# Three edits of issue order in an encoder trunk: key copies, a modulation sum, low parts of activations

## The chip, the cores and the metric

The kernel runs on one core of one Trainium2 chip. The metric is the device time of one execution in microseconds (us). The engines are TensorE (PE), VectorE (DVE), ScalarE (ACT), GpSimd (POOL) and SyncE (SP). Each works through its own instruction stream strictly in order and waits on semaphores for the others.

## The reference

Two encoder layers over 256 tokens of width 1024, float32. Every sub-layer works on a normed and modulated stream, and its output returns through a gate. Only the first layer's attention and the start of its channel mixer matter here:

```python
mod = silu(c) @ ada_w[l] + ada_b[l]
sh_a, sc_a, g_a, sh_f, sc_f, g_f = jnp.split(mod, 6, axis=-1)
h = modulate(rms_norm(x, norm_attn[l]), sh_a, sc_a)
# differential attention, 8 heads, two softmax maps each
q, k, v = split(h @ w_qkv);  q = rms_norm(q) / 8;  k = rms_norm(k)
p = softmax(q k^T + bias)                    # two maps: p[0], p[1]
o = (p[0] - lam * p[1]) @ v
y = (rms_norm(o) * (1 - lam_init)).reshape(...) @ w_o
x = x + g_a * y
h = modulate(rms_norm(x, norm_ffn[l]), sh_f, sc_f)
x = x + g_f * (silu(h @ w_in_gate) * (h @ w_in_up)) @ w_out
```

After this come a shared key and value projection, a layer of sliding-window attention and a mixture of 8 experts (top 2), which takes some two thirds of the time.

## The kernel before

**Units and split products.** All weights stream through a ring of 12 raw slots of 128x1024 float32 (`WRAW`), loaded by SP. One slot's content is a unit. ACT copies a unit, rounded, to `WHI` (`hi`, line 697) and DVE subtracts to get the low part `WLO` (`lo`, line 1080). Each product is three matmuls (`split_mm`): high by high, high by low, low by high. There are 6 split slots, so `hi(k)` waits until TensorE has used unit k-6, and a raw slot is loaded again when `lo` of its unit is done. The activations, transposed by TensorE into PSUM, are split the same way: `ht_his` on ACT (line 756), `ht_los` on DVE (line 1153 or 1155).

**Unit numbers.** 0 to 7 are the query weights, 8 to 15 key, 16 to 23 value, 24 to 31 the output weights, 32 to 35 the first input weights of the dense channel mixer, 36 to 39 the next, 40 and 41 its first output weights.

**Around the key copies.** TensorE runs value units 16 to 18, transposes the normed queries, runs 19 and 20, transposes the normed keys, runs 21, waits for all eight copies (`qkt_ready`, 8), computes the logits of heads 0 and 1, then unit 22, logits 2, unit 23, logits 3, and enters the attention (line 1931). The copies are `transposed(...)` on ACT (line 764). ACT copies the values to SBUF (line 802) once unit 23 is used; the first probabilities times values need them. On DVE, `biased(n)` (lines 1186 and 1190) adds the bias to head n's logits and takes the negated maximum; `totals(n)` (lines 1200 to 1206) forms the difference of maps. A block of queries is 128 rows; heads 0 to 7 of block 0 come first, then those of block 1. DVE also sums the modulation rows, one `early_product` per 128x1024 piece of `ada_w` (line 1094); eight of them, (3, 0) to (3, 7), give the shift of the channel mixer, of which the last two come after `lo(31)`.

**Around the shift sum.** `project_by_block` multiplies the attention output by units 24 to 31. Its order is (block, unit): (0,0) to (0,4), (1,0), (1,1), (0,5), (0,6), (0,7), (1,2) to (1,7). `between` names what TensorE does behind such a step. `shift_sum` waits for the last early product (`DVE_EARLY`) and sums the shift over partitions by a matmul with ones; ACT copies the result (`mod_rows`, line 741) ahead of `hi(32)`, the norm root of block 0 and `hi(33, 34)`. `block_out` after (0,7) releases `residual(0)` on DVE (lines 1235 and 1236), then `scaled`, `rms`, `norm` (line 1142). Behind (1,6) TensorE transposes that normed block.

**Into the channel mixer.** TensorE runs units 32 to 35 for block 0, transposes block 1's normed rows (line 1744, behind `norm(1)`), runs 32 to 35 for block 1, then 36 and 37 (`f_in_first`), transposes the activation, and goes on with 38 and 39, 40 and 41, 42 and on. POOL waits for the second half of `norm(1)` (`h_ready`, 12), clears a part of `MOD` (line 622), loads biases and a gain, and then the pieces of the later modulation matrices into the four slots of `SHR` (line 573). DVE multiplies them between its `lo` operations (`late_products`, line 1105): the first two stand ahead of `lo(38)`.

Of the kernel before, what the change touches and what calls it, by code (L numbers as in the profile page):

```python
# [20 lines left out]
ACT = mybir.ActivationFunctionType  # L21
# [30 lines left out]
U_QKV = 0  # L52
# [118 lines left out]
def trunk(nc, t):  # L171
    ctx = ExitStack()
    with ctx:
# [3 lines left out]
        def sem(name):  # L177
            return ctx.enter_context(nc.semaphore(name))
# [51 lines left out]
        K = MOD[:, 7:9, :]  # L230
# [8 lines left out]
        def s_buf(a, n):  # L239

            n = n % S_BUFS
            if a == "B":
                buf = B_BUFS[:, n * B_BUF:n * B_BUF + 2 * BIAS_COLS] if n < 3 else GB[:, 0:2 * BIAS_COLS]
                return buf.rearrange("p (m k) -> p m k", m=2)
            if n < 2:
                return S[:, n, :, :]
            return MOD[:, 5, :].rearrange("p (n m k) -> p n m k", n=2, m=2)[:, n - 2, :, :]
# [79 lines left out]
        qkt_psum = sem("qkt_psum")  # L327
# [357 lines left out]
        def _(act):  # L685
# [5 lines left out]
            def hi(u, *units):  # L691
                for k in units:
                    act.wait_ge(w_landed[u.raw(k)], u.landed(k))
                    if u.first + k >= SPLIT_SLOTS:

                        act.wait_ge(w_used, u.count(k - SPLIT_SLOTS) + 1)
                    nc.scalar.activation(WHI[:, u.split(k), :], WRAW[:, u.raw(k), :], ACT.Copy  # L697
                                         ).then_inc(w_hi, 1)
# [15 lines left out]
            def load_table(func):  # L714

                n = tables[0]
                tables[0] += 1
                nc.scalar.activation(rt[:, 7, n:n + 1], ones[:, 0:1], func)
# [42 lines left out]
            def transposed(first, dst_of, col, banks, total):  # L761
                for n, bank in enumerate(banks):
                    act.wait_ge(total, first + n + 1)
                    nc.scalar.activation(dst_of(n), PS[:, bank, :], ACT.Copy, scale=gcol[:, col:col + 1]
                                         ).then_inc(qkt_ready if total is qkt_psum else kbt_ready, 1)

            def attention(a, early=None, between=None):
                sems = attn[a]

                def exps(n):  # L770
                    i, span = n // HEADS, (n // HEADS + 1) * P
                    act.wait_ge(sems["negmax"], n + 1)
                    buf, c = s_buf(a, n), sm[:, n % S_BUFS, :]
                    cols = span if a == "A" else span + 1
                    for m in range(2):
                        nc.scalar.activation(buf[:, m, 0:cols], buf[:, m, 0:cols], ACT.Exp,
                                             bias=c[:, 2 + m:3 + m],
                                             accum_out=c[:, 4 + m:5 + m]).then_inc(sems["expd"], 1)

                def copy_pt(n):  # L780
                    maps = 1 if a == "A" else 2
                    span = (n // HEADS + 1) * P
                    act.wait_ge(sems["pt_psum"], n + 1)
                    if n >= 2:
                        act.wait_ge(sems["pv"], n - 1)
                    nc.scalar.activation(PT[:, n % 2, 0:maps, 0:span],
                                         PS[:, 4 + n % 2, :].rearrange("p (m k) -> p m k", m=2)[:, 0:maps, 0:span],
                                         ACT.Copy).then_inc(sems["pt_ready"], 1)

                def copy_o(n):  # L790
                    i, h = n // HEADS, n % HEADS
                    act.wait_ge(sems["pv"], n + 1)
                    nc.scalar.activation(Q[:, i, h * P:(h + 1) * P], PS[:, 6, 0:P], ACT.Copy,
                                         scale=sm[:, n % S_BUFS, 8:9]).then_inc(sems["o_ready"], 1)

                n_all = TB * HEADS
                exps(0)
                exps(1)
                if a == "A":
                    act.wait_ge(w_used, U_WO)  # L800
                    for i in range(TB):
                        nc.scalar.activation(V[:, i, :], pair(4 + 2 * i), ACT.Copy).then_inc(v_copied, 1)
                for n in range(n_all):
                    if n + 2 < n_all:
                        exps(n + 2)
                    copy_pt(n)
                    if n and a == "A":
                        copy_o(n - 1)
                    if n in (1, 2) and a == "B":
                        transposed(9 + n, lambda _: Q[:, 1, (n - 1) * 512:n * 512], 3, (7,), qkt_psum)  # L810
                    if n == 7 and a == "A":
                        row_half(0)
                    if n == 9 and a == "A":
                        act.wait_ge(attn["A"]["o_ready"], HEADS)
                        o_squares(0)
                    if a == "A" and n in (10, 11):
                        hi(Units(U_QKV), n + 18)
                    if a == "B" and n == 5:
                        hi(Units(U_BQ), 12)
                    if n == 13:  # L820
                        load_table(ACT.Sqrt)
                        if a == "A":
                            root(ss[:, 0, 0:8], P)
                if a == "A":
                    copy_o(n_all - 1)
# [29 lines left out]
            u = Units(U_QKV)  # L855
# [17 lines left out]
                block_squares(i, pair(2 * i), 3)  # L873
            hi(u, *range(20, 24))
            transposed(0, lambda n: Q[:, n // 2, (n % 2) * 512:(n % 2) * 512 + 512], 0, range(0, 4), qkt_psum)
            hi(u, 24, 25)
            transposed(4, lambda n: K[:, n // 2, (n % 2) * 512:(n % 2) * 512 + 512], 1, range(0, 4), qkt_psum)
            hi(u, 26, 27)
            load_table(ACT.Exp)
            attention("A")  # L880

            ht_his(1, BLOCKS[:2], gcol[:, 2:3])
# [53 lines left out]
            u = Units(U_KV - FF_OUT)  # L936
# [16 lines left out]
            u = Units(U_BQ)  # L953
# [114 lines left out]
        def _(dve):  # L1068
# [7 lines left out]
            def lo(u, *units):  # L1076
                for k in units:

                    dve.wait_ge(w_hi, u.count(k) + 1)
                    V_.tensor_tensor(WLO[:, u.split(k), :], WRAW[:, u.raw(k), :],  # L1080
                                     f32(WHI[:, u.split(k), :]), ALU.subtract).then_inc(w_lo, 1)
# [94 lines left out]
            def biased(a, n):  # L1176
                sems = attn[a]
                i, h = n // HEADS, n % HEADS
                span = (i + 1) * P
                cols = span if a == "A" else span + 1  # L1180
                dve.wait_ge(sems["logits"], n + 1)
                if n >= S_BUFS:

                    dve.wait_ge(sems["pt_psum"], n - S_BUFS + 1)
                b, buf = 2 * (n % 2), s_buf(a, n)
                V_.tensor_tensor(buf[:, :, 0:cols], PS[:, b:b + 2, 0:cols],
                                 BIAS[:, 2 * h:2 * h + 2, 2 * P - span:2 * P - span + cols], ALU.add
                                 ).then_inc(sems["biased"], 1)
                dve.wait_ge(sems["biased"], n + 1)
                V_.tensor_reduce(sm[:, n % S_BUFS, 2:4], buf[:, :, 0:cols], axis=AX, op=ALU.max, negate=True  # L1190
                                 ).then_inc(sems["negmax"], 1)
# [88 lines left out]
            u = Units(U_QKV)  # L1280
# [6 lines left out]
            def lo_and_products(k, n):  # L1287

                lo(u, k)
                for piece in islice(rest, n):  # L1290
                    early_product(piece)
# [26 lines left out]
            lo_and_products(19, (18 in GATE_AT) + (19 in SCALE_AT))  # L1318
            for k in range(20, 24):
                lo_and_products(k, (k in GATE_AT) + (k in SCALE_AT))  # L1320
            lo_and_products(24, 0)
            lo_and_products(25, 1)
            dve.wait_ge(bias_landed, 16 * TOEP_HEADS)
            dve.wait_ge(bias_masked, 1)
            biased("A", 0)
            biased("A", 1)
            lo(u, 26, 27)
            attention("A")
            def o_scale(i):

# [31 lines left out]
            scaled(1, H, MOD0[4], 2, 2)  # L1362
            rms(1)
            norm(1, H, MOD[:, MOD0[3], :])
            lo(u, 36)
            ht_los(2, BLOCKS[2:])
            lo(u, 37)

            def f_act(n):
                dve.wait_ge(silu_ready, n)  # L1370
# [33 lines left out]
            u = Units(U_KV - FF_OUT)  # L1404
# [20 lines left out]
            u = Units(U_BQ)  # L1425
# [266 lines left out]
        def _(pe):  # L1692
# [218 lines left out]
            u = Units(U_QKV)  # L1911
# [28 lines left out]
            def shift_sum():  # L1940
# [3 lines left out]

            project_by_block(Units(U_WO), 4, 4, {
                (0, 2): second_rows,
                (0, 5): shift_sum,
                (1, 6): lambda: ht_transposes(H, h_parts(2, BLOCKS[:2]))})

            def f_in_block(u, i, k):  # L1950
# [68 lines left out]
            u = Units(U_FF)  # L2019
# [30 lines left out]
            u = Units(U_KV - FF_OUT)  # L2050
# [18 lines left out]
            u = Units(U_KV)  # L2069
# [271 lines left out]
```

## Time and profile before

| what | value |
|---|---|
| median of 3 runs | 1528.77 us (1524.25, 1528.77, 1528.91) |
| the profiled execution | 1525.94 us, of it 1524.1 us span |
| PE busy | 1466.6 us (96%) |
| DVE busy | 1292.8 us (85%) |
| ACT busy | 979.9 us (64%) |
| POOL busy | 130.7 us (9%) |
| mean granted TensorE clock | 0.991 |
| chain that ended last, by engine | PE 90%, DVE 5%, ACT 2%, DMA 2%, issue 1% |

The span is the time from the first to the last recorded instruction. Where PE is busy without a gap, only fewer or faster matmuls would help; an edit of order can help only where PE is idle, or where its granted clock is low.

### The profile page before, as it was taken

Reading aid. Unit: us, or ns where it says so; the run is one execution under the profiler, and the core shown is the slowest. Engines: PE = TensorE matmul, PEld = TensorE weight load, DVE = VectorE, ACT = ScalarE, POOL = GpSimd, SP = SyncE. Lnnn points to the kernel's source line nnn. Section 1 sums busy time; section 2 is a strip of 40 time slices with the busy share of each in tenths; the row PEclk is TensorE's granted clock in tenths of the full one; section 3 lists DMA queues with packets and bytes.
Section 4 is the critical chain, followed back from the end, with each engine's and each line's share of the span. In section 5 each row is a group of like instructions: output and inputs, shape, how many; then the busy total and the mean of one; then the engine's idle time right before and its main releaser. Section 6 shows DMA issues by size and latency. Waiting matters only on the chain.

```text
span 1524.1 us, 22197 instructions
## 1 busy us (share of the span) xinstructions
PE 1466.6 (96%) x6546; PEld 1152.2 (76%) x6546; DVE 1292.8 (85%) x1383; ACT 979.9 (64%) x1249; POOL 130.7 (9%) x143
## 2 busy tenths in 40 slices
PE   6998889999999999999999999999999999999997
PEld 2774667777677678888888888888888888888885
DVE  6888779988776788898898898888889889888896
ACT  3557343444556466777777777677777777777773
POOL 3000122211119000000000000000000000000100
PEclk9999999999999999999999999999999999999999
DMA  9984489998743479999999999999999999999993
GB/s 355 371 294 148 153 296 388 384 369 299 193 152 111 152 252 361 373 374 381 366 364 382 367 360 390 364 356 391 370 361 381 371 363 372 366 360 372 396 394 121
DMA packets 212228, 494.37 MB, mean 324 GB/s; under 512 B 16433, under 2 KB 39185, under 8 KB 212177
## 3 DMA queue, kind: packets, MB, share of 16 engines
q1 hardware_dynamic: 196848, 440.46, 79.6%
q0 software_dynamic: 14528, 51.22, 9.5%
q10 hardware_dynamic: 802, 2.06, 0.4%
q8 instruction: 26, 0.43, 0.1%
q14 instruction: 24, 0.20, 0.0%
HBM read 487.13 MB, written 6.55 MB: 324 GB/s over the span
## 4 chain that ended last, share of the span: by engine, by line
PE 90%; DVE 5%; ACT 2%; DMA 2%; issue 1%; SPq 0%; DVEq 0%; ACTq 0%
PE PS L1694 87%; PE PS L2211 2%; DMA WRAW<-in_ada_w 1%; DVE MOD L1094 1%; DVE WLO L1080 1%; PE PS L1744 1%; PE PS L1817 0%; DVE HT_LO L1153 0%; PE PS L2189 0%; DMA WRAW<-in_a_w_o 0%; DVE X L1236 0%; DVE H L1235 0%; SPq L439 0%; PE PS L1994 0%; DVE ss L1160 0%
## 5 line engine op out<-in xcount | busy, mean ns | idle before, releaser
L1080 DVE TENSOR_TENSOR WLO<-WRAW,WHI 128x1024 fp32r<-128x1024 f32 x790 | 915.7, 1219 | 39.1 <-ACT WHI L697 38.5
L697 ACT ACTIVATE WHI<-WRAW 128x1024 fp32r<-128x1024 f32 x790 | 779.6, 1052 | 90.9 <-PE PS L1694 70.0
L1694 PE MATMUL PS<-WHI,HT_HI 128*128 128x512 f32 x1280 | 516.0, 403 | 9.9 <-DVE HT_LO L1153 6.4
L1694 PE MATMUL PS<-WLO,HT_HI 128*128 128x512 f32 x1280 | 508.0, 397 | 0.0
L1694 PE MATMUL PS<-WHI,HT_LO 128*128 128x512 f32 x1280 | 434.4, 396 | 0.0
L1694 PEld LDWEIGHTS PS<-WHI,HT_HI 128*128 128x128 f32 x1280 | 241.6, 189 | 67.6 <-DVE WLO L1080 7.2
L1694 PEld LDWEIGHTS PS<-WHI,HT_LO 128*128 128x128 f32 x1280 | 241.1, 188 | 58.8
L1694 PEld LDWEIGHTS PS<-WLO,HT_HI 128*128 128x128 f32 x1280 | 241.7, 189 | 55.1 <-issue 0.5
L1694 PE MATMUL PS<-WHI,AT_HI 128*128 128x512 f32 x536 | 216.7, 404 | 3.0 <-DVE AT_LO L1375 1.6
L1694 PE MATMUL PS<-WLO,AT_HI 128*128 128x512 f32 x536 | 211.7, 395 | 0.0
L1694 PE MATMUL PS<-WHI,AT_LO 128*128 128x512 f32 x536 | 211.7, 395 | 0.0
L1022 ACT ACTIVATE AT_HI<-PS 128x512 fp32r<-128x512 f32 x56 | 33.5, 599 | 197.4 <-PE PS L2211 197.4
L1694 PEld LDWEIGHTS PS<-WHI,AT_HI 128*128 128x128 f32 x536 | 100.6, 188 | 30.2 <-issue 2.2
L1694 PEld LDWEIGHTS PS<-WLO,AT_HI 128*128 128x128 f32 x536 | 100.6, 188 | 26.7 <-issue 2.9
L1694 PEld LDWEIGHTS PS<-WHI,AT_LO 128*128 128x128 f32 x536 | 100.6, 188 | 24.5
L1606 DVE TENSOR_TENSOR AT_LO<-PS,AT_HI 128x512 fp32r<-128x512 f32 x56 | 38.8, 692 | 92.7 <-ACT AT_HI L1022 92.7
L1105 DVE SCALAR_TENSOR_TENSOR MOD<-SHR,condT,MOD 128x1024 f32<-128x1024 f32 x64 | 82.0, 1281 | 4.2 <-DMA SHR<-in_ada_w 1.5
L665 POOL DMA_DIRECT2D y_rows<-MOD x7 | 4.0, 572 | 792.7 <-DVE MOD L1583 792.7
L907 ACT ACTIVATE AT_HI<-PS 128x512 fp32r<-128x512 f32 x11 | 6.6, 599 | 65.6 <-PE PS L1994 65.6
L1094 DVE SCALAR_TENSOR_TENSOR MOD<-WRAW,condT,MOD 128x1024 f32<-128x1024 f32 x32 | 41.0, 1281 | 6.1 <-DMA WRAW<-in_ada_w 5.5
L1694 PE MATMUL PS<-MOD,CST 128*128 128x512 f32 x64 | 34.8, 656 | 10.9 <-DVE MOD L1094 6.4
L1018 ACT ACTIVATE MOD<-PS 128x512 f32<-128x512 f32 x56 | 33.5, 599 | 15.3 <-PE PS L1694 15.3
(222 smaller groups left out, 860.5 us busy)
## 6 DMA issues: line engine op xcount, KB each, us to landing
WRAW<-in_moe_w_in SPq DMA_DIRECT2D x448, 512.0 KB, 6.4
WRAW<-in_moe_w_out SPq DMA_DIRECT2D x224, 512.0 KB, 5.5
WRAW<-in_ada_w SPq DMA_DIRECT2D x48, 512.0 KB, 8.8
SHR<-in_ada_w POOLq DMA_DIRECT2D x48, 512.0 KB, 6.6
WRAW<-in_ffn_w_in SPq DMA_DIRECT2D x88, 256.0 KB, 7.9
WRAW<-in_a_w_qkv SPq DMA_DIRECT2D x24, 512.0 KB, 12.9
WRAW<-in_ffn_w_out SPq DMA_DIRECT2D x22, 512.0 KB, 6.3
SHR<-in_kv_ada_w POOLq DMA_DIRECT2D x16, 512.0 KB, 6.8
```

What stands on the lines that cost most here:

```text
L665: pool.dma_start(Y_ROWS.ap()[e * P:(e + 1) * P, :], Y).then_inc(y_stored, 16)
L697: nc.scalar.activation(WHI[:, u.split(k), :], WRAW[:, u.raw(k), :], ACT.Copy).then_inc(w_hi, 1)
L907: nc.scalar.activation(AT_HI[:, :], PS[:, 2, :], ACT.Copy).then_inc(at_hi, 1)
L1018: nc.scalar.activation(ESIL, PS[:, 0, :], ACT.Silu).then_inc(e_silu, 1)
L1022: nc.scalar.activation(AT_HI[:, :], PS[:, 2, :], ACT.Copy).then_inc(e_at_hi, 1)
L1080: V_.tensor_tensor(WLO[:, u.split(k), :], WRAW[:, u.raw(k), :], f32(WHI[:, u.split(k), :]), ALU.subtract).then_inc(w_lo, 1)
L1094: V_.scalar_tensor_tensor(row, piece, condT[:, k:k + 1], row, ALU.mult, ALU.add).then_inc(ada_used, 1)
L1105: V_.scalar_tensor_tensor(row, ADA[:, k % ADA_SLOTS, :], condT[:, k:k + 1], row, ALU.mult, ALU.add).then_inc(ada_used, 1)
L1606: V_.tensor_tensor(AT_LO[:, :], PS[:, 2, :], f32(AT_HI[:, :]), ALU.subtract).then_inc(e_at, 1)
L1694: return nc.tensor.matmul(out, a, b, start=start, stop=stop)
L1744: last = nc.tensor.transpose(PS[:, 2 * i + half, k * P:(k + 1) * P], src[:, i, c:c + P], ident)
L2211: last = nc.tensor.transpose(PS[:, 2, c * P:(c + 1) * P], EACT[:, c * P:(c + 1) * P], ident)
```

## The change

Four places, no instruction added or removed:

- ACT (line 876 to 879): the four key copies and the table load for the exponential go ahead of `hi(24, 25)`; `hi(26, 27)` moves behind the exponentials of heads 0 and 1.
- DVE (lines 1321 to 1327): `biased(0)` goes ahead of `lo(24)`; the one product that stood behind `lo(25)` stands behind `lo(24)`; `lo(25)` moves behind `biased(1)`, ahead of `lo(26, 27)`.
- TensorE (line 1947): the shift sum moves from behind (0,5) to behind (1,2), past (0,6), (0,7) and (1,2).
- DVE (lines 1365 to 1367): `lo(36)` moves behind `ht_los(2, BLOCKS[2:])`, the low parts of block 1's normed rows.

```diff
@@ ScalarE, attention(a)
                 exps(0)
                 exps(1)
                 if a == "A":
+                    hi(Units(U_QKV), 26, 27)
                     act.wait_ge(w_used, U_WO)
@@ ScalarE
             transposed(0, lambda n: Q[...], 0, range(0, 4), qkt_psum)
+            transposed(4, lambda n: K[...], 1, range(0, 4), qkt_psum)
+            load_table(ACT.Exp)
             hi(u, 24, 25)
-            transposed(4, lambda n: K[...], 1, range(0, 4), qkt_psum)
-            hi(u, 26, 27)
-            load_table(ACT.Exp)
             attention("A")
@@ VectorE
-            lo_and_products(24, 0)
-            lo_and_products(25, 1)
             dve.wait_ge(bias_landed, 16 * TOEP_HEADS)
             dve.wait_ge(bias_masked, 1)
             biased("A", 0)
+            lo_and_products(24, 1)
             biased("A", 1)
-            lo(u, 26, 27)
+            lo(u, 25, 26, 27)
             attention("A")
@@ VectorE
             norm(1, H, MOD[:, MOD0[3], :])
-            lo(u, 36)
             ht_los(2, BLOCKS[2:])
-            lo(u, 37)
+            lo(u, 36, 37)
@@ TensorE
             project_by_block(Units(U_WO), 4, 4, {
                 (0, 2): second_rows,
-                (0, 5): shift_sum,
+                (1, 2): shift_sum,
                 (1, 6): lambda: ht_transposes(H, h_parts(2, BLOCKS[:2]))})
```

## Rows read from the trace of the kernel before

**Rows 1.** Windows: stretch, its length, busy us of engines, granted clock, DMA share, GB/s.
```profile
250.00:300.00 50.00, 50.00 (x210) 38.46 (x209) 46.53 (x43) 22.29 (x28) 10.60 (x20) 1.00 1.04 387
...
200.00:202.60 2.60, 2.60 (x6) 2.07 (x7) 1.87 (x3) 0.00 (x0) 2.33 (x5) 0.50 0.60 171
```

**Rows 2.** Chain of waits: start us, length us, engine and line, instructions.
```profile
199.96 12.82 PE PS L1694 x48
...
213.21 11.21 PE PS L1694 x48
```

**Rows 3.** Timeline of ACT, 98 to 120: start, length, work, [idle before and its releaser].
```profile
104.64 1.06 ACT L697 ACTIVATE WHI<-WRAW 128x1024 fp32r<-128x1024 f32 x1 [6.20 <-DMA WRAW<-in_a_w_o]
...
106.91 2.41 ACT L764 ACTIVATE MOD<-PS,gcol 128x512 f32<-128x512 f32 x4
...
111.22 1.28 ACT L718 ACT_TABLE_LOAD   x1
...
118.07 1.94 ACT L802 ACTIVATE H<-PS 128x1024 f32<-128x1024 f32 x2 [3.81 <-PE PS L1694]
```

**Rows 4.** Timeline of PE, 101 to 121.
```profile
101.70 1.91 PE L1755 MATMUL PS<-CST,MOD 128*128 128x128 f32 x16
...
109.37 0.71 PE L1694 MATMUL PS<-MOD,Q 64*128 64x128 f32 x8 [2.95 <-ACT MOD L764]
...
114.54 0.49 PE L1694 MATMUL PS<-MOD,Q 64*128 64x128 f32 x4
```

**Rows 5.** Timeline of DVE, 111 to 122.
```profile
111.89 2.35 DVE L1080 TENSOR_TENSOR WLO<-WRAW,WHI 128x1024 fp32r<-128x1024 f32 x2
115.08 0.42 DVE L1186 TENSOR_TENSOR MOD<-PS,SHR 128x256 f32<-128x256 f32 x1 [0.84 <-PE PS L1694]
...
121.72 0.42 DVE L1186 TENSOR_TENSOR S<-PS,SHR 128x256 f32<-128x256 f32 x1 [0.43 <-PE PS L1694]
```

**Rows 6.** Timeline of PE around modulation sums, 152 to 187.
```profile
152.67 1.88 PE L1694 MATMUL PS<-MOD,CST 128*128 128x512 f32 x4
...
172.70 3.44 PE L1694 MATMUL PS<-MOD,CST 128*128 128x512 f32 x4 [3.74 <-DVE MOD L1094]
```

**Rows 7.** Timeline of ACT, 176 to 183.
```profile
176.24 1.03 ACT L741 ACTIVATE MOD<-PS 128x1024 f32<-128x1024 f32 x1 [7.53 <-PE PS L1694]
...
182.69 0.29 ACT L730 ACTIVATE nx<-nx,eps 128x1 f32<-128x1 f32 x1
```

**Rows 8.** Timeline of DVE, 169 to 185.
```profile
169.89 2.67 DVE L1094 SCALAR_TENSOR_TENSOR MOD<-WRAW,condT,MOD 128x1024 f32<-128x1024 f32 x2
172.47 1.22 DVE L1125 SCALAR_TENSOR_TENSOR MOD<-MOD,S 128x1024 f32<-128x1024 f32 x1
178.98 1.23 DVE L1235 TENSOR_TENSOR H<-PS,MOD 128x1024 f32<-128x1024 f32 x1 [5.29 <-PE PS L1694]
...
183.21 1.42 DVE L1142 SCALAR_TENSOR_TENSOR H<-H,nx,MOD 128x512 f32<-128x512 f32 x2
```

**Rows 9.** Timelines of ACT, DVE and PE at the second block's rows, 195 to 200.
```profile
195.81 1.20 ACT L756 ACTIVATE HT_HI<-PS 128x512 fp32r<-128x512 f32 x2 [0.92 <-PE PS L1744]
...
197.98 1.23 DVE L1080 TENSOR_TENSOR WLO<-WRAW,WHI 128x1024 fp32r<-128x1024 f32 x1 [2.32 <-ACT WHI L697]
...
199.96 0.77 PE L1694 MATMUL PS<-WHI,HT_HI 128*128 128x512 f32 x1 [3.58 <-DVE HT_LO L1153]
```

**Rows 10.** Timelines of POOL and DVE, 195 to 224.
```profile
195.72 2.67 POOL L622 MEMSET MOD<- 128x3072 f32 x1 [30.07 <-DVE H L1142]
...
200.23 2.10 POOL L573 DMA_DIRECT2D SHR<-in_kv_ada_w  x4
...
209.85 1.28 DVE L1105 SCALAR_TENSOR_TENSOR MOD<-SHR,condT,MOD 128x1024 f32<-128x1024 f32 x1 [0.49 <-DMA SHR<-in_kv_ada_w]
...
223.16 1.22 DVE L1080 TENSOR_TENSOR WLO<-WRAW,WHI 128x1024 fp32r<-128x1024 f32 x1
```

**Rows 11.** Loads into SHR, whole span: time to landing.
```profile
DMA to landing us min/median/max: 4.9/6.8/21.9
```

More of the change, by code:

```diff
@@ L875, in _ @@
             transposed(0, lambda n: Q[:, n // 2, (n % 2) * 512:(n % 2) * 512 + 512], 0, range(0, 4), qkt_psum)
+            transposed(4, lambda n: K[:, n // 2, (n % 2) * 512:(n % 2) * 512 + 512], 1, range(0, 4), qkt_psum)
+            load_table(ACT.Exp)
             hi(u, 24, 25)
-            transposed(4, lambda n: K[:, n // 2, (n % 2) * 512:(n % 2) * 512 + 512], 1, range(0, 4), qkt_psum)
-            hi(u, 26, 27)
-            load_table(ACT.Exp)
             attention("A")
```

## The prediction

> **What bounds the kernel now.** I read the windows first. In the long stages TensorE is busy the whole stretch at full clock while DVE and ACT have room (50 of 50 us busy between 250 and 300) [rows 1]. The chain of waits says the same: 48 matmuls in 11.21 us without a break, 0.2335 us each [rows 2]. The edits touch none of that. They can only pay in idle time of TensorE between 106 and 200 us, so next I looked for those holes in the timelines. There are three. At 106.4 it waits 2.95 us for the key copies [rows 4]. At 169.0 it waits 3.74 us for the last product of the shift [rows 6]. At 196.4 it waits 3.58 us for the low parts of block 1's rows [rows 9]. Behind a hole the clock falls: granted 0.50 between 200.0 and 202.6 [rows 1], and the 48 matmuls from 199.96 take 12.82 us where 48 warm ones take 11.21: 1.6 us more [rows 2]. Whether a closed hole shortens the kernel depends on whether DVE, which stands behind each of them, comes earlier too.
>
> **Part A, key copies and biases.** TensorE transposes the keys from 101.70, and ACT could copy as they come, but ACT stands in `hi(24)` until a load lands at 104.64, then in `hi(25)`, and copies from 106.91 for 2.41 us [rows 3, 4]. Moved ahead, the copies start at about 102.3 (the first of four groups of transposes, 1.91 / 4 = 0.5 us) and end near 104.8. TensorE is then bound by unit 21, done at 106.4. So the logits of heads 0 and 1 start 2.95 us earlier, at 106.4. Unit 22 took 114.54 - 110.08 = 4.5 us behind the hole [rows 4]; 12 warm matmuls take 2.8 [rows 2]. Logits 2 come at about 109.9 instead of 114.5, unit 23 is done at 113.1 and logits 3 follow.
>
> What is late next is DVE. It loses nothing and gains nothing in work: the same four `lo`, one product and two biases, from about 107.0. Its `lo(26)` now needs `hi(26)`, which on ACT stands behind the exponentials of head 1, which need `biased(1)`: I count `biased(1)` done at 110.9, exponentials until 111.7, `hi(26)` (1.06) until 112.8, against DVE free at 112.0. That is 0.8 us of new wait. DVE reaches `biased(2)` at 115.1, just as before (115.08) [rows 5]. But the logits are there now, so the three idle gaps of DVE before the next biases (the first 0.84 and the last 0.43 us, 1.9 in all) go [rows 5]; the first of them paid for the later arrival, so 1.1 us is left at `biased(4)`. The value copies, which stood at 118.07 behind unit 23 [rows 3], run behind `hi(27)` at 113.9, so TensorE no longer waits for them. Following the loop of logits, biases and probabilities for heads 5 to 7 by hand, two more small gaps close and the lead settles at 1.5 us. Bounds: 0 (DVE as before) and 4.1 (the whole lead of the value copies, 118.07 - 113.9 [rows 3]). I take 1.5, since DVE works almost without a gap from there. The table load (1.28) [rows 3] is hidden: ACT has done it by 106.2, ahead of the logits. SP's queue: unit 28 takes the raw slot of 25, whose `lo` ends at 112.0 instead of 109.2, but that load stands in SP's queue behind pieces which wait for products up to 121 anyway, so nothing comes of it.
>
> **Part B, the shift sum.** Times here are of the trace before, without A's shift. Units 30 and 31 are split by 168.6 and 170.0, the second just ahead of the two last products, which run from 169.89 to 172.56 [rows 8]. With the sum moved back TensorE goes on at 168.8: (0,6) until 170.2, (0,7) until 171.7, (1,2) until 173.1, at 6 x 0.2335 = 1.4 us each. The products are done by then, so the sum does not wait: 1.88 us warm instead of 3.44 [rows 6]. The hole and its cold matmuls are gone: about 5.3 us for TensorE.
>
> DVE and ACT must follow. The fold runs until 173.69 [rows 8], so `residual(0)` starts there, 5.3 us ahead of 178.98. But the sum now ends at about 174.9, and ACT's queue behind it is longer than the wait was: the row copy (1.03) until 176.0, `hi(32)` until 177.0, only then the squares (1.06) and the root. The root ends at about 178.4 against 182.98 [rows 7]: 4.6 us earlier, not 5.3. So `norm(0)` ends at 180.1 instead of 184.63. TensorE reaches the transposes behind (1,6) at 180.3, just behind it. From there DVE works in a row (`lo`, low parts, residual and norm of block 1), all 4.6 us earlier. Bounds: 3.7 (the hole, less nothing else) and 5.3. I take 4.6, the place of the root.
>
> **Part C, low parts ahead of lo(36).** DVE waits 2.32 us for `hi(36)`, then works at it from 197.98, and the low parts come behind it; the high parts were there from 196.4 [rows 9]. Swapped, TensorE gets block 1's rows at 197.2 instead of 199.96, a hole of 0.9 instead of 3.58 us, and keeps its clock: 2.7 + 1.6 = 4.3 us. I cost this at nothing all the same, because what comes next doesn't move. The first two late products stand ahead of `lo(38)`, and the second waited for its load until 209.85 [rows 10]. That load is POOL's; it hangs on `norm(1)`, then the memset at 195.72, then the issues from 200.23 [rows 10], none of which C touches. So DVE still starts the second product 14.1 us behind `norm(1)`, `lo(38)` ends at 212.3, and DVE works in a row to `lo(42)`, which ends at 224.38 [rows 10]; TensorE had started on unit 42 right then. With the lead it comes to unit 38 at about 209 and waits some 3.3 us there. The hole has moved and not gone. Holes of 2.95, 3.74 and 3.58 us were each followed by slow matmuls, so I add one cold stretch of 1.6 us [rows 2]; of it about 1.1 fit into the slack ahead of `lo(42)`, and 0.5 is lost. Bounds: -4.3 (all kept) and +1.6; I take +0.5, by the row of 209.85.
>
> One rule of the Trainium skill speaks against C. The memset and POOL's first issues now run beside two more DVE operations. Four such issues ran at 200.23 in 2.10 us, with a `lo` beside them, no longer than anywhere else, and so I put no cost on it [rows 10]. The Trainium skill, "SBUF — State Buffer", section "SBUF: two separate sides", says that DVE and GpSimd share a pair of ports by an exclusive lock, and that a DVE operation that holds it keeps GpSimd from writing the descriptors of its DMAs. By that rule, if `lo` held the pair, up to two `lo` (2.4 us) would be added to C; by the row, nothing.
>
> **Sum.** 1.5 + 4.6 - 0.5 = 5.6 us. Everything later is in step with TensorE, so it should arrive at the end. Against the profiled execution: 1525.94 - 5.6 = 1520.3. The median of the runs shown is 2.8 us above that execution, and 5.6 off it gives 1523.2. I say 1522.0, between them.
>
> **Rivals.**
> - *A gives nothing* (0.17). If the new wait of `lo(26)` grows, or heads 4 to 7 turn out paced by ACT, the attention ends when it did. For it: DVE reaches `biased(2)` at the same time. Against: its idle gaps have a named cause that goes. 5.6 - 1.5 = 4.1 us: about 1523.5.
> - *The loads set the pace* (0.13). The DMA share is 1.04 between 250 and 300, at 387 GB/s [rows 1]. If the mixer ran at the rate of its loads, only what starts the loads earlier counts: that is the last early product, which moves by A alone. 1.5 - 0.5 = 1 us: about 1526.5. Against it: TensorE has no gap in that stretch.
> - *C is kept* (0.10). If the second load lands sooner than at 209.85 once TensorE is earlier, the 4.3 us of C add in full: 1.5 + 4.6 + 4.3 = 10.4 us, about 1517.
> - *The load into SHR is late* (0.05), the slower side. Place: the second piece, waited for at 209.85, 9 us after its issue. Now unit 37's `lo` comes 1.2 us earlier, so the next weight loads run against it. From 5.6 us of lateness on the gain is gone. The longest landing of any load into that tile is 21.9 us [rows 11]; that would be 12.9 us late, and 12.9 - 6.1 = 6.8 us slower: about 1534.
>
> **How the numbers follow.** 0.55 for the forecast, the others as above. The three runs shown lie 4.7 us apart, so a measured median strays by some 2 to 3 us by itself. The bound for a difference that can be told is 0.3%, 4.6 us, that is 1524.2. Of the forecast's 0.55, some 0.39 falls below it, of the first rival's 0.17 some 0.08, of the loads' nearly none, of C's all 0.10: with a little from the rest 0.58 faster. Slower gets 0.06, the rest is 0.36. The range goes from 1516.5 (C kept) to 1527.0 (the loads set the pace).
>
> **What would show it.** A right: TensorE goes from unit 21 to logits without a gap, logits 2 near 110, and `residual(0)` starts some 1.5 + 5.3 us earlier. B right: the sum takes under 2 us with no wait, and the second half of `norm(1)` ends 6.1 us earlier. C right: the hole ahead of block 1's units is under 1 us, a new one of about 3 us stands ahead of unit 38, behind a late product, and TensorE starts on unit 42 some 5.6 us earlier than at 224.5. It is wrong if a wait for a load into `WRAW` appears in the mixer, or if no hole stands ahead of unit 38.

## The result, and the profile after

The changed kernel takes 1521.49 us in the median of 11 runs (1512.04 to 1523.54), the kernel before 1526.48 (1522.66 to 1530.51, 11 runs). The ratio is 0.9957, with a 95% interval of 0.9945 to 0.997: 6.6 us less by the ratio (4.6 to 8.4), 5.0 by the medians. The forecast was 1522.0 us and 5.6 us less. The sum came out near, but not by its terms: part A gave less than I put on it, B and C more. The profiled execution after took 1523.48 us with a span of 1521.7, only 2.4 us less than before; it is one of the longest of the 11, with a mean granted clock of 0.989 where the shortest had 0.997.

**Part A.** Timeline of PE, kernel after (the line of its matmuls is 1692 now). It answers to [rows 4] and the first row of [rows 6].

```profile
106.48 0.71 PE L1692 MATMUL PS<-MOD,Q 64*128 64x128 f32 x8
...
110.13 0.49 PE L1692 MATMUL PS<-MOD,Q 64*128 64x128 f32 x4
...
117.02 0.30 PE L1815 MATMUL PS<-CST,S 128*128 128x128 f32 x1 [2.99 <-DVE S L1206]
...
154.74 3.62 PE L1692 MATMUL PS<-MOD,CST 128*128 128x512 f32 x4
```

The hole for the key copies is gone and unit 22 runs at full clock (logits 2 at 110.13). But the lead doesn't reach DVE, so TensorE waits 2.99 us further on, ahead of the first probabilities. The kernel before waited there too, for the value copies, but for 1.61 us:

```profile
120.06 0.33 PE L1817 MATMUL PS<-CST,S 128*128 128x128 f32 x1 [1.61 <-ACT H L802]
```

Behind the new hole, and once more at the end of the attention, the granted clock is low. Windows of the kernel after, clock in the third column from the end (0.50 is the lower of its two levels, 1.00 the upper, and 0.59 a mean of both):

```profile
120.00:128.60 8.60, 8.46 (x28) 4.49 (x28) 5.62 (x18) 4.49 (x19) 0.00 (x0) 0.50 0.90 332
151.50:158.50 7.00, 6.05 (x17) 3.37 (x17) 3.83 (x5) 1.74 (x7) 0.57 (x1) 0.59 0.46 145
```

About the same two stretches of the kernel before:

```profile
120.00:128.00 8.00, 7.16 (x37) 3.70 (x37) 6.58 (x20) 6.66 (x31) 0.00 (x0) 1.00 0.79 286
150.00:156.00 6.00, 4.47 (x23) 2.78 (x22) 4.11 (x7) 2.75 (x9) 0.57 (x1) 1.00 0.34 100
```

What that does to DVE, in its timeline after (compare [rows 5]):

```profile
113.01 2.36 DVE L1080 TENSOR_TENSOR WLO<-WRAW,WHI 128x1024 fp32r<-128x1024 f32 x2 [0.77 <-ACT WHI L697]
115.29 0.42 DVE L1186 TENSOR_TENSOR MOD<-PS,SHR 128x256 f32<-128x256 f32 x1
...
120.69 0.42 DVE L1186 TENSOR_TENSOR S<-PS,SHR 128x256 f32<-128x256 f32 x1
...
128.06 0.42 DVE L1186 TENSOR_TENSOR MOD<-PS,SHR 128x256 f32<-128x256 f32 x1 [1.89 <-PE PS L1692]
...
159.97 1.43 DVE L1155 SCALAR_TENSOR_TENSOR HT_LO<-PS,gcol,HT_HI 128x512 fp32r<-128x512 f32 x2 [4.38 <-ACT HT_HI L756]
```

At `biased(4)` DVE is 1.03 us ahead (120.69 against 121.72). Then it waits up to 1.89 us for logits that come slowly. With the gate sum at 3.62 us for 1.88 [rows 6], the low parts of the attention output begin at 159.97. Before, they began at 155.74:

```profile
155.74 1.41 DVE L1155 SCALAR_TENSOR_TENSOR HT_LO<-PS,gcol,HT_HI 128x512 fp32r<-128x512 f32 x2 [1.60 <-ACT HT_HI L756]
```

In this execution the attention with A ends 4.2 us later.

**Part B.** PE and DVE after, beside [rows 6 and 8]:

```profile
177.22 1.88 PE L1692 MATMUL PS<-MOD,CST 128*128 128x512 f32 x4
```

```profile
177.84 1.22 DVE L1235 TENSOR_TENSOR H<-PS,MOD 128x1024 f32<-128x1024 f32 x1
...
182.56 0.17 DVE L1117 RECIPROCAL nx<-nx 128x1 f32<-128x1 f32 x1 [0.91 <-ACT nx L730]
182.76 1.42 DVE L1142 SCALAR_TENSOR_TENSOR H<-H,nx,MOD 128x512 f32<-128x512 f32 x2
```

The sum neither waits nor runs slowly. `norm(0)` starts at 182.76, 0.45 us ahead of 183.21, though the stage began 4.2 us late: B gives 4.7 us here, and 4.9 at the norm of block 1 (193.55 against 194.24).

**Part C.** PE, POOL and DVE after, beside [rows 9 and 10]:

```profile
196.58 0.47 PE L1692 MATMUL PS<-WHI,HT_HI 128*128 128x512 f32 x1 [0.90 <-DVE HT_LO L1153]
...
210.44 0.52 PE L1692 MATMUL PS<-WHI,HT_HI 128*128 128x512 f32 x1 [1.99 <-DVE WLO L1080]
```

```profile
199.53 2.10 POOL L573 DMA_DIRECT2D SHR<-in_kv_ada_w  x4
```

```profile
207.97 1.28 DVE L1105 SCALAR_TENSOR_TENSOR MOD<-SHR,condT,MOD 128x1024 f32<-128x1024 f32 x1 [0.47 <-DMA SHR<-in_kv_ada_w]
...
221.27 1.22 DVE L1080 TENSOR_TENSOR WLO<-WRAW,WHI 128x1024 fp32r<-128x1024 f32 x1
```

The hole moved to the place forecast, ahead of unit 38 behind the second late product. It is 1.99 us and not 3.3: the product starts 8.44 us behind POOL's first issue, 9.62 before. `lo(42)` starts at 221.27, 1.9 us ahead of 223.16, of which `norm(1)` brought 0.7. From there to the end the kernel after is 1.3 to 2.4 us ahead, if the same instruction of DVE is compared in both; at the end it is 2.4.

### The profile page after: what moved, and what is told of

Read it like the earlier page. It is cut to its first block, busy times and chain, and to the rows that moved or that the text cites. A ratio compares the mean times of both kernels' runs of the same rounds, so it can differ in the third digit from the quotient of the medians.

```text
span 1521.7 us, 22197 instructions
## 1 busy us (share of the span) xinstructions
PE 1470.1 (97%) x6546; PEld 1155.0 (76%) x6546; DVE 1292.4 (85%) x1383; ACT 979.5 (64%) x1249; POOL 130.6 (9%) x143
## 4 chain that ended last, share of the span: by engine, by line
PE 89%; DVE 6%; DMA 2%; ACT 1%; issue 1%; SPq 0%; POOL 0%; DVEq 0%; ACTq 0%
PE PS L1692 85%; PE PS L2209 2%; DMA WRAW<-in_ada_w 1%; DVE WLO L1080 1%; DVE MOD L1094 1%; DMA SHR<-in_kv_ada_w 1%; PE PS L1815 0%; PE PS L1742 0%; PE PS L2187 0%; DVE HT_LO L1153 0%; DVE H L1142 0%; DVE X L1236 0%; DVE H L1235 0%; SPq L439 0%; DVE sm L1190 0%
```

## The experiments

Kernels of one group ran on one chip with the kernel before beside them. Each gives its ratio to before, with the 95% interval.

### The three parts alone

**e1, part A alone:** both of ScalarE's edits and the first of VectorE's on the kernel before (ScalarE's in part, shortened).

```diff
+            transposed(4, lambda n: K[...], 1, range(0, 4), qkt_psum)
+            load_table(ACT.Exp)
             hi(u, 24, 25)
 # with hi(26, 27), biased(0) and lo(24, 25) moved as in the change; no other edit
```

> Part A alone on the kernel before. Theory (clock): the profile after shows a new hole of 2.99 us just ahead of the attention, and behind it slow matmuls until 128 us, so A by itself gives nothing or loses: 0 to 2 us slower in the median, with a hole of about 3 us ahead of the first transpose of the probabilities in its profile and a granted clock near 0.5 behind it. Rival (my prediction): 1.5 us faster.

Measured: 0.9984 (0.9966 to 1.0002), 1525.78 us against 1527.44. That is 2.4 us less (from 0.3 more to 5.2 less). The clock theory put it at 0 to 2 us slower, of which nearly all is outside; my 1.5 us faster is inside. PE, e1:

```profile
116.61 0.45 PE L1816 MATMUL PS<-CST,S 128*128 128x128 f32 x1 [2.99 <-DVE S L1206]
116.85 1.91 PE L1693 MATMUL PS<-MOD,CST 128*128 128x512 f32 x2
...
150.94 1.88 PE L1693 MATMUL PS<-MOD,CST 128*128 128x512 f32 x4
```

The hole is there, with slow matmuls just behind it (1.91 for 1.02), but the clock is back early and the gate sum is warm, 1.7 us earlier than in [rows 6]. The gate sum's start agrees with the 1.5 us that I had put on A. How far the length of the slow stretch decides what A gives is taken up behind e11.

**e2, parts B and C without A:**

```diff
-                (0, 5): shift_sum,
+                (1, 2): shift_sum,
-            lo(u, 36)
             ht_los(2, BLOCKS[2:])
-            lo(u, 37)
+            lo(u, 36, 37)
```

> Parts B and C without A. Theory (clock): A costs, so this is as fast as the full change or faster: 5 to 8 us faster than before, no slow matmuls in the attention. Rival (A is worth 1.5 us): it gives up 1.5 us of the full change, 3.5 to 5 us faster than before.

Measured: 0.9941 (0.9919 to 0.9962), 9.0 us less. At or above the full change, as the theory had it, though the two intervals overlap; the rival's 3.5 to 5 us are outside (5.8 to 12.4). **e3, part B alone** (the shift sum's line):

```diff
-                (0, 5): shift_sum,
+                (1, 2): shift_sum,
```

> Part B alone. Theory: 4.6 us faster, set by ACT's queue behind the sum; the second half of norm of block 1 ends 4.6 us earlier than 195.6. Rival (the loads set the pace in the mixer): 0 to 1 us.

Measured: 0.9958 (0.994 to 0.9975), 6.4 us less (3.8 to 9.2). The rival of the loads is out: B passes through the mixer in full. The profile has the second half of `norm(1)` at 191.63 for 194.24, 2.6 us earlier, though the attention ended 2.3 us later in it: again 4.9 us by B. **e4, part C alone:**

```diff
-            lo(u, 36)
             ht_los(2, BLOCKS[2:])
-            lo(u, 37)
+            lo(u, 36, 37)
```

> Part C alone. Theory after the profile: the hole of 3.6 us ahead of block 1's units is replaced by one of about 2 us ahead of unit 38, whose end is set by the second load into SHR; TensorE starts on unit 42 about 1 us earlier than at 224.5. 0 to 1.5 us faster. My prediction: 0.5 us slower. Rival (C is kept): 4.3 us faster.

Measured: 0.9983 (0.9967 to 0.9998), 2.6 us less (0.3 to 5.0). PE, e4:

```profile
200.54 0.47 PE L1693 MATMUL PS<-WHI,HT_HI 128*128 128x512 f32 x1 [0.91 <-DVE HT_LO L1153]
...
214.29 0.50 PE L1693 MATMUL PS<-WHI,HT_HI 128*128 128x512 f32 x1 [1.88 <-DVE WLO L1080]
```

3.58 us of hole become 0.91 and 1.88. The forecast of 0.5 us slower is outside the interval. The time alone does not rule out the rival's 4.3 us; the second hole does, and the profile gives 1.3 us between `norm(1)` and `lo(42)`. B and C alone add up to what both give (6.4 + 2.6 = 9.0). A's 2.4 us are not seen on top of them in the full change (6.6), but the intervals are too wide to show that A does not add.

The profiles without A show something that one trace could not. PE of e2 and of e3, then ACT of e3:

```profile
109.98 1.23 PE L1693 MATMUL PS<-MOD,Q 64*128 64x128 f32 x8 [3.43 <-ACT MOD L764]
```

```profile
110.45 1.23 PE L1694 MATMUL PS<-MOD,Q 64*128 64x128 f32 x8 [4.13 <-ACT MOD L764]
```

```profile
107.03 1.06 ACT L697 ACTIVATE WHI<-WRAW 128x1024 fp32r<-128x1024 f32 x1 [1.72 <-DMA WRAW<-in_a_w_o]
```

The hole that A closes is not 2.95 us but 2.95 to 4.13 in the five profiles without A, by when the load of unit 25 lands (ACT waited 0.24 us for it in [rows 3], 1.72 here). The logits themselves run slowly too (1.23 for 0.71).

### What holds A back, and what C left

**e5, the full change and a filled hole:**

```diff
             project(u, 2 * KT, 4, range(7, 8))
+            pe.wait_ge(attn["A"]["biased"], 2)
+            for _ in range(3):
+                mm(PS[:, 3, :], ones, CST[:, 0:512])
             logits("A", 3)
```

> The full change, and three matmuls whose result nobody reads between unit 23 and logits 3, in the time in which TensorE would otherwise wait 3 us ahead of the attention. They add 2.6 us of work into a hole of 3.0. Theory (the clock behind the hole takes back what A gives): no slow matmuls in the attention, the sum of the gate behind it at about 57.4 us behind the split of unit 19 as in the profile of the copies alone, and 2 to 4 us faster than the full change, 9 to 10.5 us faster than before. Rival (the slow stretches come from elsewhere, or cost nothing): the same as the full change, 5 to 7 us faster than before.

Measured: 0.9942 (0.992 to 0.9963), 8.9 us less (5.6 to 12.2). That is not told apart from the full change (8.7 in its repetition, e9). PE, e5:

```profile
113.30 2.74 PE L1692 MATMUL PS<-CST 128*128 128x512 f32 x6
...
116.88 0.30 PE L1815 MATMUL PS<-CST,S 128*128 128x128 f32 x1 [0.42 <-DVE S L1206]
...
152.18 3.42 PE L1692 MATMUL PS<-MOD,CST 128*128 128x512 f32 x4
```

The hole is 0.42 us and the first slow stretch is gone, but the gate sum still ran slowly, where TensorE waits again and again for the last heads. There are two slow stretches, and the filling takes away one. The theory was right on the first stretch and wrong on the gate sum and on what the filling is worth.

**e6, the full change, `lo(38, 39)` ahead of the first late products:**

```diff
+                if step == 0:
+                    lo(u, 2, 3)
                 for k in range(4):
-                    if step or k >= 2:
+                    if step:
                         lo(u, k0 + k)
                     late_products(1)
```

> The full change, and in the mixer's first step the low parts of units 38 and 39 ahead of the first two late products. Theory (the hole of 2 us ahead of unit 38 is the second load into SHR and nothing else): the hole goes, unit 42 starts 1.5 to 2 us earlier against the end of norm of block 1, 2 us faster than the full change. Rival (DVE's work up to unit 42 sets the pace whatever the order): unit 42 starts when it did, the hole stands ahead of 42, no gain.

Measured: 0.9949 (0.993 to 0.9969), 7.8 us less, not told apart from the full change. PE, e6:

```profile
214.17 0.47 PE L1694 MATMUL PS<-WHI,AT_HI 128*128 128x512 f32 x1 [0.43 <-DVE WLO L1080]
...
221.02 0.47 PE L1694 MATMUL PS<-WHI,HT_HI 128*128 128x512 f32 x1 [1.02 <-DVE WLO L1080]
```

No hole ahead of unit 38; in its place 0.43 us ahead of unit 40 and 1.02 ahead of 42. Against the start of `norm(1)` unit 42 comes 27.8 us behind (221.02 - 193.23), in the full change 29.05 (222.60 - 193.55): 1.3 us gained, not 1.5 to 2. Both the theory (the load causes the hole) and the rival (DVE's work sets the pace next) hold in part. Part of what is left is the loads again: DVE waits 0.50, 0.55 and 0.26 us for the second, third and fourth piece in `SHR`.

**e7, the full change, the gate sum moved into the attention:**

```diff
                     if a == "A":
                         scale_pieces(n)
+                        if n == 14:
+                            mod_sums(DVE_QKV, MOD0[2], 2)
             attention("A", 4)
-            mod_sums(DVE_QKV, MOD0[2], 2)
```

> The full change, and the sum of the gate rows (1.9 us of matmuls warm, 3.6 cold) moved from behind the attention to behind the products of head 13, where TensorE waits for DVE and ACT. Theory (the chain there is DVE and ACT, TensorE has room): the first transpose of the attention output comes about 1.7 us earlier, 1.5 to 2 us faster than the full change; more where the clock was low. Rival: it delays the transposes of the last heads by as much, no gain.

Measured: 0.9938 (0.9918 to 0.9958), 9.5 us less. PE, e7:

```profile
148.97 1.88 PE L1692 MATMUL PS<-MOD,CST 128*128 128x512 f32 x4
152.07 0.68 PE L1692 MATMUL PS<-H,W 128*128 128x128 f32 x4 [0.55 <-ACT Q L793]
152.59 1.04 PE L1742 MATMUL PS<-CST,Q 128*128 128x128 f32 x8
```

The sum is done while ACT works on the last heads, and the transposes follow the last product at once, at 152.59; the full change had them at 158.15 in its profile, where the clock was low. The time isn't told apart from that of the full change.

**e8, all three additions.** The edits of e5, e6 and e7 together (shown in part):

```diff
+            for _ in range(3):
+                mm(PS[:, 3, :], ones, CST[:, 0:512])
+                if step == 0:
+                    lo(u, 2, 3)
+                        if n == 14:
+                            mod_sums(DVE_QKV, MOD0[2], 2)
```

> The full change with all three additions. If each closes a hole of its own they add: 2 to 4, 2 and 1.7 us on top of the full change, 12 to 14 us faster than before. If DVE's row of work from the attention to the mixer takes some of it back, 8 to 10 us.

Measured: 0.9912 (0.9889 to 0.9935), 1513.44 us in the median against 1526.88, 13.4 us less (9.9 to 16.9), all four runs between 1511.02 and 1514.91. The granted clock was 1.00 from 94 to 230 us in its profile.

### What A is worth

**e9, the full change once more** (no edit):

```diff
 # the change as shown, nothing added
```

> The full change once more, beside the next two on one chip. If the key copies (A) are worth what they give in mean over executions, it is 5 to 8 us faster than before.

Measured: 0.9943 (0.9925 to 0.9961), 8.7 us less. The interval (6.0 to 11.5) overlaps that of the first result (4.6 to 8.4). Its gate sum was slow again. PE, e9:

```profile
152.31 3.16 PE L1692 MATMUL PS<-MOD,CST 128*128 128x512 f32 x4
```

**e10, e8 without A and without the filling.** Of the edit against e8, ScalarE's part alone is shown, in part; VectorE's part of A is undone too, and the three filling matmuls are out:

```diff
-            transposed(4, lambda n: K[...], 1, range(0, 4), qkt_psum)
-            load_table(ACT.Exp)
             hi(u, 24, 25)
+            transposed(4, lambda n: K[...], 1, range(0, 4), qkt_psum)
+            hi(u, 26, 27)
+            load_table(ACT.Exp)
```

> Parts B and C, the gate sum early and the low parts of unit 38 first, but not A and no filling matmuls. Theory (A's gain is real once its hole is filled: the hole behind late loads, 3 to 4 us, stays here, with slow matmuls in unit 22): 2.5 to 4 us slower than the version with everything, 9.5 to 11 us faster than before. Rival (A is worth nothing in itself, the loads only move the wait): as fast as everything, 13 us faster.

Measured: 0.9934 (0.9921 to 0.9947), 10.1 us less (8.1 to 12.1). The rival's 13 us are outside.

**e11, e8 without the filling alone:**

```diff
-            pe.wait_ge(attn["A"]["biased"], 2)
-            for _ in range(3):
-                mm(PS[:, 3, :], ones, CST[:, 0:512])
```

> The full change with the gate sum early and the low parts of unit 38 first, without the filling matmuls. Theory (the slow matmuls behind A's hole are the cost of it, in some executions only): runs spread wider than with the filling, from the same best to 5 us above, 1.5 to 3 us slower in the median than with everything. Rival (filling does nothing): the same 13 us.

Measured: 0.9907 (0.9893 to 0.9921), 14.2 us less, 1513.96 us in the median, four runs from 1512.07 to 1514.18. So the filling is worth nothing here that can be seen, and the theory that it would be 1.5 to 3 us fell. PE of e11:

```profile
148.54 3.21 PE L1694 MATMUL PS<-MOD,CST 128*128 128x512 f32 x4
```

The early gate sum itself was slow in it, 3.21 us, and the transposes behind it start at 153.49.

e10 and e11 differ in A alone. Every run of e11 (1512.07 to 1514.18) is shorter than every run of e10 (1516.40 to 1519.14); the medians lie 3.5 us apart, and the two intervals touch (8.1 to 12.1 us and 12.1 to 16.3). But their profiles don't lay this on A. PE of e10 (its key hole and the start of unit 42) and of e11 (unit 42):

```profile
109.23 0.71 PE L1695 MATMUL PS<-MOD,Q 64*128 64x128 f32 x8 [3.00 <-ACT MOD L764]
...
217.51 0.47 PE L1695 MATMUL PS<-WHI,HT_HI 128*128 128x512 f32 x1 [1.00 <-DVE WLO L1080]
```

```profile
216.36 0.47 PE L1694 MATMUL PS<-WHI,HT_HI 128*128 128x512 f32 x1 [1.01 <-DVE WLO L1080]
```

At unit 42 e11 is 1.15 us ahead, and that by a later landing of the second piece in `SHR` in e10 (a hole of 1.80 us for 0.61 ahead of unit 40). The spans are 1517.3 and 1512.1, so the other 4 us arise behind unit 42, where the two kernels are alike. The windows of e10 and e11 show the clock there:

```profile
480.00:560.00 80.00, 74.01 (x363) 58.23 (x362) 56.26 (x87) 41.29 (x54) 11.30 (x8) 0.96 0.54 185
```

```profile
480.00:560.00 80.00, 74.94 (x374) 59.81 (x375) 60.25 (x88) 43.55 (x55) 11.30 (x8) 1.00 0.60 201
```

So the difference of the runs is real, but that it is A's is not shown.

All 13 profiles together say more. DVE's work from `lo(22)`, which no edit moves, to the first bias of the second block of queries, `biased(8)`, holds all that A moves; from there to the low parts of the attention output lies the gate sum. DVE of the kernel before, of the kernel after, and of e9, which is the same kernel as after:

```profile
102.18 1.22 DVE L1080 TENSOR_TENSOR WLO<-WRAW,WHI 128x1024 fp32r<-128x1024 f32 x1
...
129.00 0.69 DVE L1186 TENSOR_TENSOR S<-PS,SHR 128x512 f32<-128x512 f32 x1 [0.38 <-PE PS L1694]
```

```profile
102.33 1.22 DVE L1080 TENSOR_TENSOR WLO<-WRAW,WHI 128x1024 fp32r<-128x1024 f32 x1
...
130.46 0.69 DVE L1186 TENSOR_TENSOR S<-PS,SHR 128x512 f32<-128x512 f32 x1 [0.81 <-PE PS L1692]
```

```profile
102.15 1.22 DVE L1080 TENSOR_TENSOR WLO<-WRAW,WHI 128x1024 fp32r<-128x1024 f32 x1
...
127.52 0.69 DVE L1186 TENSOR_TENSOR S<-PS,SHR 128x512 f32<-128x512 f32 x1 [0.39 <-PE PS L1692]
```

| profiles | `lo(22)` to `biased(8)`, us | `biased(8)` to the low parts, us |
|---|---|---|
| before, e2, e4, e3 (no A) | 26.82, 28.27, 28.91, 29.23 | 26.74, 26.73, 26.73, 26.74 |
| e1 (A, gate sum at full clock) | 25.36 | 26.74 |
| e9, e5 (A, gate sum slow) | 25.37, 25.38 | 29.14, 29.25 |
| after, e6 (A, clock low until 128, gate sum slow) | 28.13, 27.90 | 29.51, 29.76 |
| e10 (no A, gate sum early) | 26.86 | 25.90 |
| e7, e8 (A, gate sum early) | 25.37, 25.38 | 25.92, 25.91 |
| e11 (A, gate sum early but slow) | 25.38 | 27.59 |

Three things follow. The forecast lead of 1.5 us is there in six of the eight profiles with A (25.4 against 26.8), with the new hole filled (e5, e8) or open (e1, e7, e9, e11): DVE sets the pace, so a short slow stretch of TensorE costs nothing, and filling the hole gives nothing. Where the clock stayed low until 128, the lead is gone. And a slow gate sum behind the attention costs 2.4 to 3.0 us, about as much as A brings; inside the attention the slow one costs 1.7 us, and a fast one is worth 0.8.

## Why the prediction was right or wrong

- *Part A, DVE's side.* Right in every step that was counted: logits at 106.5, logits 2 at 110.1, the new wait of `lo(26)` 0.77 us (0.8 forecast), `biased(2)` no earlier, 1.0 us ahead at `biased(4)` (1.1 forecast).
- *Part A, "the lead settles at 1.5 us" and arrives at the end.* The lead was right: 1.45 us in six of eight profiles. The step that failed is the path from there, on which I left out the clock. I wrote that DVE is late next, and did not write down what that leaves TensorE: 3 us with nothing to do, as long as the hole that was closed. I priced a hole of C at a cold stretch and left out this one. The loop of logits, biases and probabilities ran at half clock in the profile (0.50 from 120 to 128.6), which took the lead in two of eight profiles, and the gate sum behind it took 3.62 us for 1.88. With A and the gate sum in its old place the sum was slow in four of five profiles (after, e5, e6 and e9; warm in e1); without A in none of four (before, e2, e3, e4). That A makes the second stretch more likely is a count over nine profiles, and its cause was not shown; the stretch appears in e5 too, where the first hole is filled.
- *Part A, what it removes.* Undersized. The hole hangs on a load, 2.95 us in the trace I had, 4.13 and 4.08 in e3 and e4. Up to `biased(8)` the profiles without A take 28.0 us in mean, those with A and a short slow stretch 25.4: 2.6 us. A alone gives 2.4 us in the runs (0.3 more to 5.2 less). In the full change, beside B and C, it gives nothing that can be told (6.6 and 8.7 us with A, 9.0 without).
- *Part B.* Right in mechanism: no wait, 1.88 us, and ACT's queue (row copy, `hi(32)`, squares, root) sets `norm(0)`, with a wait of 0.91 us for the root on DVE. 4.6 us forecast, 4.7 to 4.9 in the profiles, 6.4 (3.8 to 9.2) alone.
- *Part C.* The place was right and the size wrong. The lead ends at unit 38 behind the second load into `SHR`. But the hole there is 1.3 to 2.0 us and not 3.3, since that product starts 8.44 us behind POOL's first issue and not 9.62; so 1.2 us is gained in the profile (1.3 in those of e2 and e4), and 2.6 (0.3 to 5.0) by the runs of e4, where I had put a loss of 0.5. Why the load lands sooner is open. It came 9.62, 9.63 and 9.60 us behind POOL's first issue in before, e1 and e10, and 7.74 to 8.45 in the nine others that wait for it; e10 has the edit of C, so C alone is not the reason. The slow matmuls that I priced behind the new hole came in after, e2 and e4 (0.50) and not in e5 and e7 (1.00), behind holes of 1.87 to 1.99 us in all five, and `lo(42)` came 1.2 to 1.3 us sooner behind `norm(1)` in each: DVE sets the pace there, and they cost nothing.
- *Rivals.* The loads set the pace: ruled out by e3. C is kept in full: no. The load into `SHR` is late: no. A gives nothing: the nearest to what the full change shows, for the reason above. The total was right since B and C gave more than I put on them and A less, and that is luck.
- *The rule of the Trainium skill* ("SBUF — State Buffer", "SBUF: two separate sides"): POOL's three issues from 197.98, beside the moved `lo(36)` and `lo(37)`, took 0.52, 0.49 and 0.55 us (before 0.52, 0.50 and 0.55), and the four into `SHR` 2.10 us as before. The trace shows none of the lock there.

## What to carry to other kernels

When an edit closes a hole of TensorE, find where the next hole opens: a lead that the next engine can't use comes back as a wait elsewhere. Then ask who sets the pace behind it. Slow matmuls beside a busy DVE cost nothing here (25.4 us with and without them); in the chain at the end of the attention they cost 2.4 to 3.0 us. Small sums and other work without a deadline belong inside a stage that waits for other engines, not behind it, where they stand in the chain and run on a low clock. A wait for a load has a spread: one trace gives one draw of it. And when two runs differ, compare them where their kernels are alike too: 4 of the 5.2 us between the profiles of e10 and e11 arose there.

## What the runs showed of the hardware that was not expected

The executions of one kernel spread by 9 us (1522.33 to 1531.11 in 26 runs of before), and the spread follows the mean granted clock: 0.994 in the fastest of them and 0.988 in the slowest, with 1.4 us per 0.001 by a straight line through all 26. The changed kernel's best of 11 runs was 1512.04 us at 0.997, its slowest 1523.54 at 0.989. Windows show where it goes: from 560 us on the clock is 1.00 in every profile, so the difference lies in the stages ahead of that, and part of it between 400 and 560, which no edit touches (e10 and e11 above). In one and the same kernel a hole of 2.99 us was followed by slow matmuls until 128.6 us in the profile after and until about 121 in e9: 0.68 and 0.89 in mean over the 16 us from 114. A hole of 1.9 us was followed by 0.50 or by 1.00. So what follows a hole differs from execution to execution, with the same instructions in the same order. What decides how long it stays low was not settled.

The fastest version is the change with the gate sum inside the attention and the low parts of units 38 and 39 first (e8, e11), 13 to 14 us under the kernel before.
